# Six filler products at each of six seams of a two-block transformer kernel are taken out

## The reference

```python
for layer in range(DEPTH):                                  # DEPTH = 2
    h = h + 0.5 * rmsnorm(swiglu(rmsnorm(h, g[0]), w_ffn_in[layer, 0], w_ffn_out[layer, 0]), g[1])
    hn = rmsnorm(h, g[2])
    mix = gla_mixer(...) if layer < N_A_LAYERS else swa_mixer(...)
    h = h + rmsnorm(mix, g[3])
    h = h + 0.5 * rmsnorm(swiglu(rmsnorm(h, g[4]), w_ffn_in[layer, 1], w_ffn_out[layer, 1]), g[5])
    if layer == N_A_LAYERS - 1:
        k_sh, v_sh = shared_kv(h, kv_norm, w_kv, cos, sin)
...
proj = h @ w_in[l] + b_in[l]                                # second block, one layer
y_a = hgrn2_mixer(...) @ w_proj_a[l]
y_b = moba_mixer(...) @ w_proj_b[l]
mixed = (sigmoid(gate_a) * y_a + sigmoid(gate_b) * y_b) @ w_out[l]
x = layer_norm(DN_ALPHA * h + mixed, ...)
x = layer_norm(DN_ALPHA * x + hier_moe(x, ...), ...)        # 32 experts, the best 2 of one group
```

## Time and profile before

| | |
|---|---|
| median of 3 runs | 1772.81 us (1772.8 to 1776.44) |
| profiled execution, its own time | 1771.16 us |
| its span, first to last instruction | 1769.2 us |
| TensorE products busy | 1729.7 us, 98% |
| VectorE, ScalarE busy | 1057.2 us, 725.4 us |
| mean granted TensorE clock | 0.994 |

### The profile page before, as it was taken

One profiled execution on the slowest core, in us unless ns is written; L12 is line 12 of the kernel. 1 busy time (PEld: TensorE's weight loads), 2 busy tenths in 40 slices (PEclk: granted clock), 3 DMA queues, 4 the chain that ended last, 5 costly groups with the idle time before them and its releaser, 6 DMA issues.

```text
span 1769.2 us, 31464 instructions
## 1 busy us (share of the span) xinstructions
PE 1729.7 (98%) x12356; PEld 1401.2 (79%) x12356; DVE 1057.2 (60%) x1915; ACT 725.4 (41%) x1175; POOL 21.2 (1%) x26
## 2 busy tenths in 40 slices
PE   9999999999999999999999999999999999999997
PEld 8999989899999999997899999998953333333332
DVE  7775566687755877569787656867662222222223
ACT  6444462464444544456654436957421101110110
POOL 0000000100000000000000001000020000000000
PEclk9999999999999999999999999999999999999999
DMA  6545334445553355532245545443879999999996
GB/s 246 184 180 192 126 132 155 60 143 190 186 199 138 143 178 180 206 129 93 96 168 195 219 168 190 147 152 120 333 309 426 426 427 428 427 429 427 427 427 258
DMA packets 42340, 409.71 MB, mean 232 GB/s; under 512 B 5304, under 2 KB 5304, under 8 KB 7056
## 3 DMA queue, kind: packets, MB, share of 16 engines
q1 hardware_dynamic: 40032, 402.21, 58.3%
q0 software_dynamic: 1936, 5.79, 1.6%
q10 hardware_dynamic: 288, 0.52, 0.1%
HBM read 405.87 MB, written 2.63 MB: 231 GB/s over the span
## 4 chain that ended last, share of the span: by engine, by line
PE 84%; DMA 6%; DVE 6%; ACT 2%; issue 1%; SPq 0%; DVEq 0%; ACTq 0%
PE ps L599 82%; PE ps L603 2%; DMA branch<-w_gate_up 2%; DMA late<-w_gate_up 2%; DMA raw<-w_units 2%; DMA soon<-w_gate_up 1%; DVE w_lo L1775 1%; ACT w_hi L1306 1%; DVE h L1889 0%; DVE branch L1817 0%; DVE x_lo L1840 0%; ACT arena L1547 0%; DVE x_lo L1838 0%; ACT arena L1564 0%; DVE h L1893 0%
## 5 line engine op out<-in xcount | busy, mean ns | idle before, releaser
L599 PE MATMUL ps<-x_hi,w_hi 128*128 128x256 f32 (+1 forms) x2144 | 614.1, 286 | 8.2 <-DVE x_lo L1838 3.6
L599 PE MATMUL ps<-x_lo,w_hi 128*128 128x256 f32 (+1 forms) x2144 | 610.2, 285 | 0.0
L599 PE MATMUL ps<-x_hi,w_lo 128*128 128x256 f32 (+1 forms) x2144 | 608.8, 284 | 0.0
L1775 DVE TENSOR_TENSOR w_lo<-raw,w_hi 128x1024 fp32r<-128x1024 f32 (+1 forms) x352 | 448.5, 1293 | 138.3 <-ACT w_hi L1306 137.0
L1306 ACT ACTIVATE w_hi<-raw 128x1024 fp32r<-128x1024 f32 (+1 forms) x352 | 385.3, 1114 | 208.0 <-PE ps L599 132.0
L599 PEld LDWEIGHTS ps<-x_hi,w_hi 128*128 128x128 f32 x2144 | 403.6, 188 | 15.1 <-issue 7.7
L599 PEld LDWEIGHTS ps<-x_hi,w_lo 128*128 128x128 f32 x2144 | 405.5, 189 | 0.0
L599 PEld LDWEIGHTS ps<-x_lo,w_hi 128*128 128x128 f32 x2144 | 404.5, 189 | 0.2
L599 PE MATMUL ps<-hid_hi,w_hi 128*128 128x272 f32 (+1 forms) x720 | 206.0, 286 | 0.8 <-DVE hid_lo L1840 0.4
L599 PE MATMUL ps<-hid_hi,w_lo 128*128 128x272 f32 (+1 forms) x720 | 204.6, 284 | 0.0
L599 PE MATMUL ps<-hid_lo,w_hi 128*128 128x272 f32 (+1 forms) x720 | 204.0, 283 | 0.0
(11 more groups left out here) (337 smaller groups left out, 1989.6 us busy)
## 6 DMA issues: line engine op xcount, KB each, us to landing
raw<-w_units SPq DMA_DIRECT2D x144, 1024.0 KB, 4.8
soon<-w_gate_up SPq DMA_DIRECT2D x32, 2048.0 KB, 22.0
late<-w_gate_up SPq DMA_DIRECT2D x24, 2048.0 KB, 21.3
raw<-w_out_units SPq DMA_DIRECT2D x32, 1408.0 KB, 6.2
soon<-w_down SPq DMA_DIRECT2D x16, 2048.0 KB, 25.0
late<-w_down SPq DMA_DIRECT2D x12, 2048.0 KB, 22.4
branch<-w_gate_up SPq DMA_DIRECT2D x8, 2048.0 KB, 23.0
branch<-w_down SPq DMA_DIRECT2D x4, 2048.0 KB, 20.8
```

The source lines that it names most:

```text
L599: return nc.tensor.matmul(out_ap, lhsT, rhs, start=start, stop=stop, skip_group_check=True)
L1775: v.tensor_tensor(part(w_lo, c, 0, n), raw_slot(u, j * n, n), part(w_hi, c, 0, n).bitcast(F32), ALU.subtract).then_inc(lo_made, 1)
```

## The change

The loop that issues the six filler products goes from `stat_end`. Nothing else in the program is changed; lines below it move up by three.

```diff
                 pe.wait_ge(sq_made, 8 * (n // 2 + 1))
                 mm(ps[t[0]][:, 0:w], C("ones"), sq[:, 1, 0:w], False, True).then_inc(full[t[0]], 1)
-
-                for _ in range(6):
-                    mm(ps[6][:, 0:w], C("ones"), C("cos", 0, w), True, True)
```

## The result

The changed kernel takes 1781.62 us, the median of 6 runs (1779.58 to 1783.82); the kernel before, on the same chip, 1773.45 (1772.8 to 1776.44). The ratio is 1.0043 with a 95% interval of 1.0031 to 1.0055: 8.2 us slower. (Ratio and interval are worked out from the runs and not from the two medians, so that they can differ a little from the medians' quotient, here 1.0046.) The profiled execution has a span of 1779.2 us where before had 1769.2.

A forecast was written before the change was run, and what follows sets the result against it. The prediction took TensorE, busy 98% of the span, as the bound. Seam losses of 5.6 + 1.0 + 0.1 = 6.7 us gave 1777.9 on the profiled time, 1779.5 on the median; forecast 1779.0, own range 1777 to 1781.5, overall 1773.0 to 1784.5.

The forecast's parts named there:

- The cause: At all six seams: removing fillers gains 0 directly, but leaves TensorE idle 3.0 to 4.8 us, so its clock falls.
- The mean granted clock: Sign to look for over the whole run: TensorE's mean clock falls from 0.994 to about 0.988 through six stretches at half clock.
- The price of one whole stretch: Behind a seam: 3.4 us at half clock, wholly on work, loses 1.52 us (256 columns) or an estimated 1.53 (272).
- How much of a stretch falls on work: At a seam: an early fall spends part of its stretch waiting, leaving 1.27 us lost, or 0.54 at the sixth.
- The early bound: Earliest fall in a gap taken as 2.56 us after TensorE's last product, as at the program's end.
- The term of the four full seams: Seams 1, 2, 4 and 5, with TensorE at full pace behind them: 1.4 us lost each, 5.6 in all.
- that of the sixth: Sixth seam, idle 4.76 us: 0.54 to 1.52 us lost, taken as 1.0.
- the sum of 6.7: Loss over all six seams: 5.6 + 1.0 + 0.1 us, with ends of 5.6 and 8.1.
- longer falls: Rival at five seams: a second half-clock stretch follows, costing up to 1.5 us more each; 14 us, 1787; chance 0.07.
- The third seam: TensorE waits 1.75 us for VectorE's tiles behind it, covering the loss: 0 to 0.5 us, taken as 0.1.
- the gaps pass at full clock: Rival at the seams: the clock stays at 1.00 through the idle 3.0 us, nothing lost; 1771 to 1774; chance 0.13.
- The fillers were in the way: Rival at the seams: fillers delay the first product; removal gains up to 0.4 us each, 1770 to 1771; chance 0.02.

The follow-up runs named there:

- second profile: The same code as the changed kernel, run once more and profiled again; 1783.13 us against 1774.6 for the kernel before, ratio 1.0047.
- e2_third: Against the kernel before: the six fillers given up at the third seam alone, kept at the other five; 1773.53 us against 1772.9, ratio 0.9991.
- e1_thin: Against the kernel before: fillers as many and as long, but using 16 of the 128 rows; 1782.99 us against 1772.9, ratio 1.0052.
- e7_columns: Against the kernel before: fillers keep 128 rows but use 16 of the fixed operand's 128 columns; 1772.83 us against 1774.6, ratio 1.0001.
- e5_nine: Against the kernel before: nine fillers at each seam instead of six; 1774.42 us against 1774.6, ratio 1.0001.
- e6_more: Against the kernel before: ten fillers at the sixth seam, four more ahead of the last product stage, one ahead of the 16-row products; 1770.89 us against 1774.6.

## Why the prediction was right

**The cause** was right and is shown. The fillers are no link of the chain and gave nothing back when they went, the gaps kept their length, the clock fell at all six seams in both profiles of the changed kernel, and 16-row fillers of about the same length bring a loss of the same size with falls at the same six seams, while 16-column fillers bring neither. The mean granted clock went to 0.985 where 0.988 was forecast; the three second stretches, 10.2 us at half clock, account for it.

**The price of one whole stretch** was right: forecast 1.52 us for 256 columns and 1.53, estimated, for 272; measured 1.53 and 1.55 at the fourth and fifth seam (256 columns), and 1.53 at the first (272) in the second profile. The estimated slow pace of 272 columns, 0.227 us, is what the trace after has (nine products from 217.29 to 219.33, rows of the order of time). By the rule of the Trainium skill, "TensorE: Matmul & The Clock Gate", section Terms, the estimate is 1.7; the measurement decides for 1.53.

**How much of a stretch falls on work** is the step that failed. I priced a fall that comes early in the gap below one that comes late: 1.27 us, and 0.54 at the sixth seam, because part of the stretch is spent waiting. That a part is spent waiting was right; that nothing follows was not. The early bound was wrong too: I took 2.56 us after the last product as the earliest point, and the fall came 1.6 us after the sum at the first seam and 1.3 us at the second seam of the second profile, with more of the stretch inside the gap and a larger loss all the same. Where the fall came 0.67 us or more ahead of the first product, a second stretch followed, all of it on work, in each such case of these profiles; at 0.33 us or less, or behind the product, none did. With an empty gap and no cover behind it, the early fall costs 2.2 to 2.8 us and the late one 1.4 to 1.55. The term of the four full seams, 5.6, measured 6.8 and 7.9; that of the sixth, 1.0, measured 2.5 both times; the sum of 6.7 is 9.7 and 10.3. I had the mechanism as a rival, *longer falls*, and gave it 0.07, because all stretches amid work in the trace of before end after 3.4 us. Those rows did not speak to it: in the one shown, TensorE worked through the whole stretch.

**The third seam** was right in kind: forecast 0.1 with an end at 0.5, measured 0.36 and 0.0, and 0.62 with the other fillers in place.

**The number** came near the time in part by luck. The forecast was 1779.0, the time 1781.62, a little above the forecast's own range of 1777 to 1781.5, though the sum was 3 us short of the trace. The two profiled executions differ by 10.0 us and the medians only by 8.2: the profiled one of before was 2.3 us below its median, that of the changed kernel 0.5. The forecast had allowed for a fall at the sixth seam in some executions of before, and e2_third shows one with the same fillers; that this is what makes the 1.8 us was not shown.

**The rival "the gaps pass at full clock"** is excluded: at all twelve gaps of the two profiles the clock fell, within the gap or at most 1.42 us behind it. The stretch of 1072.82 to 1075.18, on which it stood, passes in one execution and not in another: the clock fell behind the same wait in e2_third, with the same fillers. **"The fillers were in the way"** is excluded too: with nine of them 0.6 to 0.75 us are lost at four seams in the trace, and with six nothing, since the gaps were as long without them.

## What to carry to other kernels

## What the runs showed of the hardware that was not expected

The clock fell amid products as well as behind idleness, where these had few rows. In the profile after, the fall at 240.91 comes 1.36 us after the first of the gate's eight records with 16 rows, when six of them had begun; 0.72 us of idleness stand ahead of them. The rows are from the order of time and the time table (length, then busy time and records of PE, PEld, DVE, ACT, POOL, then clock, DMA share, GB/s):

```profile
239.55 2.63 PE L599 MATMUL ps<-arena,par 16*128 16x272 f32 x8 [0.72 <-DVE arena L1985]
```

```profile
237.50:240.90 3.40, 2.67 (x17) 2.26 (x16) 3.15 (x9) 2.70 (x6) 0.00 (x0) 1.00 0.00 0
240.91:244.31 3.40, 3.40 (x13) 2.58 (x12) 2.92 (x5) 3.03 (x4) 0.00 (x0) 0.50 0.00 0
```

TensorE was busy for 2.67 of the 3.40 us ahead of the fall. What part the 0.72 us had is not shown here, and the profile of before has no fall at its eight records. In e1_thin, where only the rows of the fillers differ from before, the clock fell at six places; in e7_columns, with few columns in place of few rows, at none.

Falls elsewhere come and go between executions of one kernel: before has four (822, 1228, 1283, 1300), e5_nine two (826, 1232), e6_more two (821, 1299), each not counting the fall behind its last products. At 1.2 and 1.5 us for the stretches at 1300 and 1283, this is of the size of the spread of before, 1769 to 1778 us over 27 runs; that it is the whole of the spread was not shown.
